# A two-layer trunk with expert retrieval: pieces of the next front dealt over the gather slots by load instead of by number

## The reference

```
h = rms_norm(x) ; proj = h @ w_in            # 6 blocks of 512 columns and a rank-16 gate
mix = [differential attention (4 heads), gated linear attention (4 heads, chunks of 64)]
x = x + mix @ w_out
h = rms_norm(x) ; q = h @ w_q                # 8 heads x 2 books of 128
s = q . sub_keys ; top 16 of 128 per book ; top 16 of the 16 x 16 sums -> 16 experts a head
gate = softmax(best) ; act = gelu(h . u_tab[expert])
x = x + sum over 8 heads x 16 experts of gate * act * v_tab[expert]
```

## Time and profile before

| | |
|---|---|
| median of three runs | 3281.9 us |
| the profiled execution | 3277.48 us, span 3275.7 us |
| mean granted TensorE clock | 0.944 of full speed |
| busy in the span | PE 2674.0 us (82%), DVE 2236.5 (68%), POOL 2178.2 (66%), ACT 750.7 (23%) |
| moved | 1185.41 MB, of it 1073.87 MB by gathers |

### The profile page before, as it was taken

The page is one execution under the profiler, slowest core; times in us unless marked ns, Lnnn a source line. Parts: engine busy times, 40 slices in busy tenths (PEclk is TensorE's granted clock), DMA queues, the critical chain, the costliest instruction groups (busy, mean ns, idle before and its releaser), DMA issues.

```text
span 3275.7 us, 26155 instructions
## 1 busy us (share of the span) xinstructions
PE 2674.0 (82%) x7328; PEld 1257.3 (38%) x7328; DVE 2236.5 (68%) x4922; ACT 750.7 (23%) x1676; POOL 2178.2 (66%) x2074
## 2 busy tenths in 40 slices
PE   7876678998987858998888777899888787777778
PEld 3444333344444423343435433344435443222223
DVE  1549974569759995467858997457966997444443
ACT  2321121223221221223222112122322121111111
POOL 0024677777776677777776677777776666777775
PEclk9888889999999989999999989999999898999999
DMA  5248999999999999999999999999999999999998
GB/s 190 78 147 297 335 351 400 406 407 371 372 403 380 338 352 388 406 406 407 377 385 385 358 362 352 407 406 406 372 374 406 360 358 357 409 409 410 409 409 328
DMA packets 351442, 1185.41 MB, mean 362 GB/s; under 512 B 37666, under 2 KB 38212, under 8 KB 351044
## 3 DMA queue, kind: packets, MB, share of 16 engines
q0 software_dynamic: 294912, 1073.87, 85.1%
q1 hardware_dynamic: 56388, 109.88, 9.0%
HBM read 1181.52 MB, written 2.10 MB: 361 GB/s over the span
## 4 chain that ended last, share of the span: by engine, by line
DVE 25%; POOL 23%; DMA 18%; PE 16%; issue 16%; ACT 1%; DVEq 0%; POOLq 0%
POOL v_ring L479 11%; POOL u_ring L479 11%; DMA u_ring<-in_peer_u,experts 10%; PE peer_acc L1275 8%; DMA v_ring<-in_peer_v,experts 8%; DVE u_ring L1003 5%; PE act_bank L1062 4%; DVE work L763 2%; DVE work L752 2%; DVE xs L1013 2%; PE dve_banks L1062 1%; DVE work L760 1%; DVE work L749 1%; DVE work L942 1%; DVE work L944 1%
## 5 line engine op out<-in xcount | busy, mean ns | idle before, releaser
L1275 PE MATMUL peer_acc<-v_ring,diag 128*128 128x512 f32 x3712 | 1826.7, 631 | 540.1 <-DMA v_ring<-in_peer_v,experts 282.9
L479 POOL DMA_INDIRECT u_ring<-in_peer_u,experts x1024 | 1094.6, 1069 | 583.6 <-issue 300.6
L479 POOL DMA_INDIRECT v_ring<-in_peer_v,experts x1024 | 1078.1, 1053 | 497.9 <-issue 241.2
L1003 DVE SCALAR_TENSOR_TENSOR u_ring<-u_ring,h 128x1024 f32<-128x1024 f32 x768 | 941.3, 1226 | 558.0 <-DMA u_ring<-in_peer_u,experts 543.6
L1275 PEld LDWEIGHTS peer_acc<-v_ring,diag 128*128 128x128 f32 x3712 | 692.0, 198 | 1559.3 <-issue 860.9
L680 ACT ACTIVATE diag<-ident,wts 128x128 f32<-128x128 f32 x928 | 339.9, 396 | 1142.5 <-PE peer_acc L1275 928.0
L1003 DVE SCALAR_TENSOR_TENSOR u_ring<-u_ring,dve_banks 128x1024 f32<-128x1024 f32 x256 | 312.6, 1221 | 253.9 <-DMA u_ring<-in_peer_u,experts 251.3
L1062 PE MATMUL act_bank<-w_ring,hT 128*128 128x512 f32 x768 | 348.5, 601 | 0.7 <-ACT hT L519 0.7
L1062 PEld LDWEIGHTS act_bank<-w_ring,hT 128*128 128x128 f32 x768 | 148.9, 195 | 190.1 <-issue 188.8
L1149 PE MATMUL act_bank<-hT,w_ring 128*128 128x256 f32 x768 | 173.9, 381 | 0.0
L1149 PEld LDWEIGHTS act_bank<-hT,w_ring 128*128 128x128 f32 x768 | 147.2, 192 | 38.6 <-issue 20.7
(11 more groups left out here) (161 smaller groups left out, 1596.1 us busy)
## 6 DMA issues: line engine op xcount, KB each, us to landing
w_ring<-in_w_in SPq DMA_DIRECT2D x24, 2048.0 KB, 18.8
w_ring<-in_peer_w_q SPq DMA_DIRECT2D x16, 2048.0 KB, 18.3
w_ring<-in_w_out SPq DMA_DIRECT2D x8, 2048.0 KB, 18.9
u_ring<-in_peer_u,experts POOLq DMA_INDIRECT x1024, 9.9
v_ring<-in_peer_v,experts POOLq DMA_INDIRECT x1024, 9.8
xs<-in_x SPq DMA_DIRECT2D x4, 512.0 KB, 7.1
keysT<-in_peer_sub_keys SPq DMA_DIRECT2D x2, 1024.0 KB, 16.6
out<-xs SPq DMA_DIRECT2D x4, 512.0 KB, 6.8
```

The source lines that it names most:

```text
L479: pool.indirect_dma_start(ring[:, n % depth, :], None, table, bass.IndirectOffsetOnAxis(ap=experts[:, tile % TILES, e:e + 1], axis=0),).th ...
L1003: tell(nc.vector.scalar_tensor_tensor(out=row, in0=row, scalar=1.0, in1=h, op0=ALU.mult, op1=ALU.mult, accum_out=dots[:, c % 2, s:s + 1]), ...
L1275: ins = nc.tensor.matmul(peer_acc[:, j * 512:(j + 1) * 512], diag[:, (v_count(c, s) - 1) % DIAGS, :], v_ring[:, n % V_RING, j * 512:(j + 1 ...
```

## The change

Each piece gets a load (a small integer): norm 1, a half product 2, a step 0, 1 or 2 by its place, the five pieces of a routed tile 3, 4, 5, 4 and 6. A front has 336 such units, 176 of them in routing. After slot n as many pieces are done as fit under `(n + 1) * 336 // 256` units beyond the first 101 pieces, with two units more for each of the first 16 slots. The pieces, their order and what each engine does in them stay as they are. So do the 101 pieces that run alone, and the v sum.

```diff
-LEAD = 10
+LEAD_SLOTS = 16
+LEAD_LOAD = 2
...
+    PRODUCT_LOAD = 2
+    ROUTE_LOADS = (3, 4, 5, 4, 6)
...
-    PARTS = NORM_PARTS + MID_STEPS + sum(PRODUCT_PARTS) + ROUTE_PARTS
-
-    PARTS_ALONE = PARTS - ROUTE_PARTS + ROUTE_TILE
+    PARTS_ALONE = NORM_PARTS + MID_STEPS + sum(PRODUCT_PARTS) + ROUTE_TILE
+
+    def front_loads():
+
+        loads = [1] * NORM_PARTS
+        for p in range(MID_STEPS):
+            loads += [PRODUCT_LOAD] * PRODUCT_PARTS[p]
+            loads.append(0 if p < QK_AT + 2 else 1 if p < ATTN_AT else 2)
+        return loads + [ROUTE_LOADS[p % ROUTE_TILE] for p in range(ROUTE_PARTS)]
+
+    FRONT_LOAD = sum(front_loads())
+    PART_ENDS = list(itertools.accumulate(front_loads() * FRONTS))
...
-            done = 0
+            done = PARTS_ALONE
...
-                due = min(n + 1, LEAD) + (n + 1) * PARTS // (HALF * PH * SLOTS)
-                for _ in range(due - done):
-                    next(parts, None)
-                done = due
+                due = (PART_ENDS[PARTS_ALONE - 1] + LEAD_LOAD * min(n + 1, LEAD_SLOTS)
+                       + (n + 1) * FRONT_LOAD // (HALF * PH * SLOTS))
+                while done < len(PART_ENDS) and PART_ENDS[done] <= due:
+                    next(parts)
+                    done += 1
                 slot_v(c, s)
```

More of the change, by code:

```diff
@@ L11 @@
+import itertools
 import math
```

## The result

The changed kernel takes 3261.0 us (median of five runs, 3257.23 to 3268.68) against 3281.3 of the kernel before (five runs, 3272.65 to 3284.26): ratio 0.9946, 95% interval 0.9928 to 0.9964. It is faster, by 20 us where 87 were forecast. The profiled execution has a span of 3255.4 us, 20.3 less than before.

What follows compares the result with a forecast made beforehand. No one engine bounds the kernel: DVE the routing, DMA the pure gathers, POOL a third limit. First period -35, middle -18, third -17, last 96 slots -17: 3281.9 - 87 = 3195 us, range 3122 to 3274.

Steps and rivals of the forecast that it cites:

- Routing: Routing spread to 132 slots: 2.80 us a slot, between rows at 2.66 and 2.93, 370 us a period.
- Rival A: Routing: POOL's issue of gathers holds slots at 2.93 us; 3244 us in all, or 3282; chance 0.19.
- The ends: First 16 slots, with twelve routing pieces, take 63 us; last 96 slots with routing, all DMA, take 249 us.
- Norm to query: Norm to query on 124 slots instead of 181: 383 us together, from 371 by DMA plus PE and ACT.
- The 2.4%: Norm to query: the old 181 slots' overrun of the DMA time, applied again to take 362 us to 371.
- PE's 7 us: 16 slots from slot 96: PE's half products and v slots take 58 us against 52 by DMA, 7 rounded up.
- ACT's 5: First four products: emptying ahead of the diagonal PE wants makes PE stand 1.2 us each, 5 us in all.
- rival B: Norm to query: PE falls back, POOL stops; 425 us there, 3321 in all; slower from 412; chance 0.10.
- Experts and weights: Routed tiles and moved weight blocks come in time or are covered; four expert waits, 23.9 us, go; nothing charged.
- no loss from the clock: Start of the products: granted clock 0.88 in the routing and 0.96 after it; no loss taken.

Runs made afterwards that it cites:

- e4_psum: Changed kernel with h of the u rows copied to PSUM for every tile, PSUM bank rings two deep instead of three: 3258.57 us, control e5_banks.
- e1_half: Changed kernel with two of the four matmuls of each half product of the projection left out (numbers mean nothing): 3188.19 us.
- e2_later: Changed kernel with ACT's emptying of the first four products of the projection one step later: 3244.11 us.
- e10_room: Changed kernel with loads redealt: attention to first output product on 58 slots instead of 44, routing on 119 instead of 132: 3239.03 us.
- e3_route85: Changed kernel with load 2 for every routing piece: routing on 85 slots, products on 52, attention on 62: 3251.99 us.
- e9: Changed kernel with three DVE operations of the attention (row maximum, two scalings) cut to 32 columns (numbers mean nothing): 3245.69 us.
- e11: e9 with DVE's mask sums and ACT's exponentials on 32 columns too (numbers mean nothing): 3232.4 us.
- e5_banks: Changed kernel with two PSUM banks in each ring instead of three, the control for e4_psum: 3297.97 us.
- e6_norm: Changed kernel with load 4 instead of 1 for each of the five norm pieces, norm on slots 91 to 104: 3277.76 us.

## Why the prediction was wrong

*Routing* was right: 370.4 us measured in the middle period for 370 forecast, 2.81 us a slot for 2.80, DVE busy for 313.36 (85%, as forecast) and 398 GB/s. Some of that was luck: 2.80 was the middle between two rows, and the reason given does not hold, as 90% does not lie between 62 and 88. Rival A, at 2.93, did not come, and e4_psum shows why not: the length of the gathers is worth 6 us there. So the measured time lies near A's 3244, but not by A's way.

*The ends* were right: 62.8 for 63 and 250.8 for 249 us.

*Norm to query* is the step that failed: "124 x 2.59 + 41 = 362 us by DMA, and with the 2.4% of before 371", then 383 with PE and ACT. It took 402.3, 400.2 and 405.4 us. 19.3 + 17.2 + 22.4 = 59 us of the 67 missing are here. Of these 59 the attention has 35, output and query 16, the small plain loads beside the eight blocks 5, the products 3. The 2.4% were a mean over the 181 slots of one front, in which the products were 3 us over in 211, the attention 2 in 155, output and query 7 in 133. I carried it over as if it went with the time. The stretches do not compress alike:

- Products: PE's 7 us and ACT's 5, and a share of the 2.4% of 3, were priced; 15.1, 13.5 and 19.1 came. They came over 37 slots rather than 16, and e1_half (under 5 left) and e2_later (8 to 12 left) confirm both causes.
- Attention: it had only its share of the 2.4%, some 3 us in 124. It was 17.3, 11.6 and 14.9 over. e10_room and e3_route85 show that this follows from the slots it is given, e9 and e11 that DVE and ACT work is about half of it, e5_banks that free banks matter. I had written its new density (9.4 slots a step to 7.6) into rival B and put no term for it into the sum. The two fronts beside the one I read, with the attention 8 to 9 over, would have been a warning.
- Output and query: 6 to 9 over where some 3 were priced, against 5, 7 and 4 before. e4_psum shows the bound here: POOL's issue, which I had weighed for the routing alone.

*Rival B* had the place and the sign of the mechanism: waits of POOL for PE. At 400 to 405 us norm to query stayed just under the 412 from which B decides for slower, and so ate most of the gain. I had B as an outcome by itself, at 0.10, when it was a matter of degree that also belonged into the forecast. The rest is spread: 6 in the first period's routing (796.5 - 62.8 - 402.3 = 331 for 325), 2 each in the third's and in the last 96 slots, less 2 by which the first slot came earlier.

*Experts and weights* were set at nothing. In the two later periods the waits of u rows for experts did go, from 8.0 us each to 0.3 and 1.3; one of 4.3 came up in the last 96 slots. In the first period stands one of 12.4 us, ahead of the u rows of slot 16; POOL's row (start, us, ... idle before and its end):

```profile
307.60 1.80 POOL L494 DMA_INDIRECT u_ring<-in_peer_u,experts  x1 [12.41 <-DVE experts L991]
```

The forecast had the third routed tile end in slot 9, wanted in slot 10. By the formula that holds for fronts 1 to 3; in front 0, whose units in advance come only slot by slot, it ends in slot 13. The wait lies in the 16 slots that DVE bounds anyway (60.25 of 62.80 us), so its time is not a sum to add. The 116 routing slots behind it took 331 us against 327 and 329 for the same slots of the later periods, so it can be worth 4 us at most. The blocks land sooner than before.

Two counts were off without moving the sum: a front has twelve weight blocks, not eight and three, so that four land in the routing, 362 us by DMA and still under 370; and in the table of slots half product 10 stands in slot 90 before, not 82.

## What to carry to other kernels

Where DMA bounds most of a kernel, each stretch that another engine bounds is a net loss, and what counts is the sum of the excesses over the DMA time. A change that deals out slots only moves excess from one stretch to another unless every stretch keeps enough slots for its own limit: here 52 slots were enough for 20 half products (1 to 4 us over) and 37 were not (14 to 19 over), and the attention was still 5 to 9 us over on 58 or 62. Before a mean is carried to a new density, split it by kind of work, look at it in more than one front, and ask of each part which engine it would meet first.

## What the runs showed of the hardware

A gather keeps POOL busy for 0.97 us on average in the routing when the u rows' second input lies in PSUM and for 1.10 when it lies in SBUF (e4_psum, e5_banks). The mean hides two kinds. In the routing of the kernel after, 170 of 261 gathers take under 1.0 us and 41 take over 1.4; 37 of these end 0.81 us after a u row that ended while they ran, as in these two rows. In e4_psum 6 of 261 are that long.

```profile
1861.92 1.22 DVE L1018 SCALAR_TENSOR_TENSOR u_ring<-u_ring,h 128x1024 f32<-128x1024 f32 x1
...
1862.41 1.55 POOL L494 DMA_INDIRECT v_ring<-in_peer_v,experts  x1 [0.30 <-issue]
```

After the norm, where PE had been busy for about half of the time, its first two v slots took 5.85 us instead of the usual 3.60 (the row at 1320.98 us); the granted clock stood at its lower level, 1.2 GHz, from 1318.6 to 1325.3 us:

```profile
1318.60:1325.30 6.70, 4.54 (x7) 1.85 (x6) 4.68 (x9) 1.85 (x5) 5.36 (x5) 0.50 0.90 304
```

The forecast took no loss from the clock there. The loss is 2.2 us in this period. e6_norm, with a granted clock of 0.95 over its norm stretch, was longer all the same.
